# One kernel of two transformer blocks: buffers moved to multiples of 128 bytes, the context's weights kept 64 bytes further on

## The reference, cut to what matters

```python
for l in range(DEPTH):                       # first block, x is (1, 512, 1024)
    h = rmsnorm(x, mix_norm[l]); p = h @ w_in[l]
    ... attention, pool_mixer, sg_mixer ...
    x = x + mix @ w_o[l]
    h = rmsnorm(x, ffn_norm[l])
    x = x + (silu(h @ w_gate[l]) * (h @ w_up[l])) @ w_down[l]
...
for l in range(DEPTH):                       # second block, ctx is (1, 256, 1024)
    y_ctx, y_lat = mixer_ab(...) if l % 2 == 0 else mixer_c(...)
    x = x + g1 * rmsnorm_2(y_lat, norm_g[l, 1])
    x = x + g2 * rmsnorm_2(swiglu(modulate(x, ...), ffn_w_in[l], ffn_w_out[l]), norm_g[l, 3])
    if l < DEPTH - 1:
        ctx = ctx + ...                      # the same two steps for the context
```

## Time and profile before

| | |
|---|---|
| median of 3 runs | 3122.15 us (3119.57 to 3127.41) |
| profiled execution, its own time | 3127.66 us |
| its span, first to last instruction | 3125.9 us |
| instructions | 41566, of them 16448 matmuls |
| mean granted TensorE clock | 0.987 of full speed |
| TensorE busy | 3051.4 us, 98% of the span |

### The profile page before, as it was taken

The page is one execution under the profiler, slowest core; times in us unless marked ns, Lnnn a source line. Parts: engine busy times, 40 slices in busy tenths (PEclk is TensorE's granted clock), DMA queues, the critical chain, the costliest instruction groups (busy, mean ns, idle before and its releaser), DMA issues.

```text
span 3125.9 us, 41566 instructions
## 1 busy us (share of the span) xinstructions
PE 3051.4 (98%) x16448; PEld 2544.5 (81%) x16448; DVE 1718.9 (55%) x2894; ACT 1188.3 (38%) x1834; POOL 1237.6 (40%) x584
## 2 busy tenths in 40 slices
PE   8999999999999999999999999999999999999999
PEld 7658888887589888778888998878888789878887
DVE  4645676845563653665337866666675457441113
ACT  4543222235544432324336655542123435432222
POOL 4214444532157333334344454444444330144442
PEclk9999999999999999999999999999999999999999
DMA  8204554622135222223333333445553210123331
GB/s 131 64 28 123 174 160 126 197 71 64 45 109 170 85 83 88 79 70 101 115 101 98 116 112 108 135 131 166 184 156 118 89 59 10 41 71 101 98 94 68
DMA packets 480434, 323.88 MB, mean 104 GB/s; under 512 B 102520, under 2 KB 447744, under 8 KB 479728
## 3 DMA queue, kind: packets, MB, share of 16 engines
q1 hardware_dynamic: 475472, 309.60, 33.9%
q10 hardware_dynamic: 2656, 6.30, 0.5%
q0 software_dynamic: 2112, 5.32, 0.5%
HBM read 315.90 MB, written 5.24 MB: 103 GB/s over the span
## 4 chain that ended last, share of the span: by engine, by line
PE 90%; DVE 6%; ACT 2%; issue 1%; POOL 1%; DMA 0%; DVEq 0%; ACTq 0%; POOLq 0%
PE G L2950 13%; PE G L2959 12%; PE G L2960 12%; PE G L2964 12%; PE G L3179 6%; PE G L3180 6%; PE G L3184 6%; PE G L2977 3%; PE G L4082 1%; PE G L3396 1%; PE SS L3307 1%; PE G L3386 1%; PE G L3733 1%; PE G L3333 1%; PE MM L3307 1%
## 5 line engine op out<-in xcount | busy, mean ns | idle before, releaser
L756 POOL TENSOR_TENSOR WL<-raw,WH 128x1024 fp32r<-128x1024 f32 (+1 forms) x520 | 1194.5, 2320 | 1760.7 <-ACT WH L827 1760.5
L827 ACT ACTIVATE WH<-raw 128x1024 fp32r<-128x1024 f32 (+1 forms) x520 | 492.5, 995 | 597.4 <-PE G L3184 404.6
L2959 PE MATMUL G<-hH,WH 128*128 128x512 f32 x1520 | 595.1, 392 | 0.7 <-ACT xtok L1559 0.7
L2960 PE MATMUL G<-hL,WH 128*128 128x512 f32 x1520 | 591.9, 389 | 0.0
L2964 PE MATMUL G<-hH,WL 128*128 128x512 f32 x1520 | 359.9, 389 | 0.0
L2959 PEld LDWEIGHTS G<-hH,WH 128*128 128x128 f32 x1520 | 285.4, 188 | 61.4 <-ACT xtok L1559 0.9
L2964 PEld LDWEIGHTS G<-hH,WL 128*128 128x128 f32 x1520 | 285.3, 188 | 59.2
L2960 PEld LDWEIGHTS G<-hL,WH 128*128 128x128 f32 x1520 | 285.5, 188 | 58.5
L1755 DVE SCALAR_TENSOR_TENSOR acc<-adaw,cvec,acc 128x512 f32<-128x512 f32 x280 | 281.9, 1059 | 4.2
L1779 DVE TENSOR_TENSOR FH<-silu,G 128x512 fp32r<-128x512 f32 x44 | 30.3, 688 | 245.7 <-PE G L2964 191.2
L2950 PE MATMUL G<-hH,WH 128*128 128x512 f32 (+1 forms) x416 | 161.3, 388 | 0.0
(11 more groups left out here) (826 smaller groups left out, 6113.6 us busy)
## 6 DMA issues: line engine op xcount, KB each, us to landing
raw<-ffn_w_in_in SPq DMA_DIRECT2D x264, 256.0 KB, 3.4
adaw<-ada_w_in SPq DMA_DIRECT2D x48, 1024.0 KB, 5.3
raw<-ab_w_in_in SPq DMA_DIRECT2D x128, 256.0 KB, 3.0
raw<-ffn_w_out_in SPq DMA_DIRECT2D x96, 256.0 KB, 3.0
raw<-w_gate_in SPq DMA_DIRECT2D x88, 256.0 KB, 3.4
raw<-w_up_in SPq DMA_DIRECT2D x88, 256.0 KB, 3.4
raw<-w_down_in SPq DMA_DIRECT2D x64, 256.0 KB, 2.9
raw<-w_in_in SPq DMA_DIRECT2D x40, 256.0 KB, 3.4
```

The source lines that it names most:

```text
L756: nc.gpsimd.tensor_tensor(WL[c % 2][:, cut], raw[c % 2][:, cut], WH[c % 2][:, cut].bitcast(F32), ALU.subtract)\
L827: nc.scalar.activation(WH[c % 2][:, cut], raw[c % 2][:, cut], ACT.Copy).then_inc(weights_hi, 1)
L2959: mm(dst, view(WH[c % 2], k), high, start=(k == 0 and not (joint and i)), stop=False)
L2960: mm(dst, view(WH[c % 2], k), low, start=False, stop=False)
```

## The change

Three things are done to places, and none to the work or to its order.

1. `WH[0]`, `WH[1]` and `WL[0]` get 32 more columns (128 bytes a partition), `WL[1]` 16 more (64 bytes). All that `keep` places behind them moves: `WH[1]` by 128 bytes, `WL[0]` by 256, `WL[1]` by 384, and `sq`, `ht`, `rstd`, `ncol`, `ident` and all the others by 448.
2. The arena is rounded up to 128 in place of 64: it starts at 130176 = 1017 x 128. All in it moves by 448 bytes and now starts on a multiple of 128. The pass `m` and `xtok` are placed 128 bytes further on in it. `sq`, `ht` and `rstd` now start 64 past a multiple of 128, `ident` on one.
3. The chunks of all passes whose name begins with c or k (`c.ab`, `c.ab12`, `c.ab13`, `c.gu`, `c.dn`, `c.o`, `k.kv`) are written by ScalarE and GpSimd, and read by TensorE, 16 columns (64 bytes) further on in `WH` and `WL`. `raw` is used as before.

```diff
+APART = 32
...
-        WH = [keep(f"WH{s}", [P, SLOT], F32R) for s in range(2)]
-        WL = [keep(f"WL{s}", [P, SLOT], F32R) for s in range(2)]
+        WH = [keep(f"WH{s}", [P, SLOT + APART], F32R) for s in range(2)]
+        WL = [keep(f"WL{s}", [P, SLOT + APART // (1 + s)], F32R) for s in range(2)]
...
-        arena = (cursor[0] + 63) // 64 * 64
+        arena = (cursor[0] + 127) // 128 * 128
...
-        PM = Pass("m", T, lasting)
+        PM = Pass("m", T, lasting + 128)
...
-        xtok, _ = lay(lasting + 28 * 1024, ("xtok", [P, 4, D], F32))
+        xtok, _ = lay(lasting + 28 * 1024 + 128, ("xtok", [P, 4, D], F32))
...
+        beside = {first[name] + i for name, n, _ in names if name[0] in "ck" for i in range(n)}
+
+        def high(c):
+            return WH[c % 2][:, APART // 2:APART // 2 + SLOT] if c in beside else WH[c % 2][:, 0:SLOT]
+
+        def low(c):
+            return WL[c % 2][:, APART // 2:APART // 2 + SLOT] if c in beside else WL[c % 2][:, 0:SLOT]
...
-                        nc.gpsimd.tensor_tensor(WL[c % 2][:, cut], raw[c % 2][:, cut], WH[c % 2][:, cut].bitcast(F32), ALU.subtract)\
+                        nc.gpsimd.tensor_tensor(low(c)[:, cut], raw[c % 2][:, cut], high(c)[:, cut].bitcast(F32), ALU.subtract)\
...
-                    nc.scalar.activation(WH[c % 2][:, cut], raw[c % 2][:, cut], ACT.Copy).then_inc(weights_hi, 1)
+                    nc.scalar.activation(high(c)[:, cut], raw[c % 2][:, cut], ACT.Copy).then_inc(weights_hi, 1)
...
-                return lambda k: (view(WH[c % 2], k), view(WL[c % 2], k))
+                return lambda k: (view(high(c), k), view(low(c), k))
```

More of the change, by code:

```diff
@@ L2957, in streamed @@
                     for k in range(K):
-                        high, low = X(k)
-                        mm(dst, view(WH[c % 2], k), high, start=(k == 0 and not (joint and i)), stop=False)
-                        mm(dst, view(WH[c % 2], k), low, start=False, stop=False)
+                        xh, xl = X(k)
+                        mm(dst, view(high(c), k), xh, start=(k == 0 and not (joint and i)), stop=False)
+                        mm(dst, view(high(c), k), xl, start=False, stop=False)
                 pe.wait_ge(weights_lo, 2 * c + 2)
@@ L2963, in streamed @@
                     for k in range(K):
-                        last = mm(dst, view(WL[c % 2], k), X(k)[0], start=False, stop=(k == K - 1 and not (joint and i == 0)))
+                        last = mm(dst, view(low(c), k), X(k)[0], start=False, stop=(k == K - 1 and not (joint and i == 0)))
                     last.then_inc(pe_done, did("pe", mark))
@@ L3169, in lowered @@
             def lowered(c, outs, count, X, lows, joint=False):
-                part = lambda w, k, cols, o: w[c % 2][:, k * cols + o:k * cols + o + P]
+                part = lambda w, k, cols, o: w[:, k * cols + o:k * cols + o + P]
                 pe.wait_ge(weights_hi, 2 * c + 2)
@@ L3177, in lowered @@
                         for k in ks:
-                            high, low = X(k)
-                            mm(dst, part(WH, k, cols, o), high, start=(k == 0 and not (joint and i)), stop=False)
-                            mm(dst, part(WH, k, cols, o), low, start=False, stop=False)
+                            xh, xl = X(k)
+                            mm(dst, part(high(c), k, cols, o), xh, start=(k == 0 and not (joint and i)), stop=False)
+                            mm(dst, part(high(c), k, cols, o), xl, start=False, stop=False)
                 pe.wait_ge(weights_lo, 2 * c + 2)
@@ L3183, in lowered @@
                     for k in range(count):
-                        last = mm(dst, part(WL, k, cols, o), X(k)[0], start=False, stop=(k == count - 1 and not (joint and i == 0)))
+                        last = mm(dst, part(low(c), k, cols, o), X(k)[0], start=False, stop=(k == count - 1 and not (joint and i == 0)))
                     last.then_inc(pe_done, did("pe", mark))
```

## The result

| | before | after |
|---|---|---|
| median of 5 runs each | 3124.67 us (3119.57 to 3134.85) | 3144.93 us (3142.44 to 3147.52) |
| ratio | | 1.0051, 95% interval 1.0030 to 1.0072 |
| span of the profiled execution | 3125.9 us | 3142.9 us |
| mean granted TensorE clock | 0.987 | 0.986 |

The kernel became slower by 0.5%, where 0.4% faster was forecast (the quotient of the two medians alone is 1.0065, inside the interval of the ratio). The granted clock is nearly the same, 0.987 and 0.986; by an estimate from these figures that could be some 3 us, not 17. The page of the kernel after: the span; each engine's busy time; the chain's shares.

What follows compares the result with a forecast made beforehand. TensorE, busy 98% of the span, was taken as the bound, its pace set by operand places. 5.0 + 1.3 + 6.8 = 13.1 us gained, from the runs' median 3122.15 to 3109.0 us; range 3101 to 3122 us.

Steps and rivals of the forecast that it cites:

- the first reading: TensorE's matmul groups split by operand places modulo 128: 512 columns fastest both at 0, 256 columns fastest 64 bytes apart.
- what stays as it is: `cH`, latents' chunks over `hH`, `k.kv`, transposes, narrow products and the other engines: no gain or loss, 0 us.
- slot 1 is worse off: Rival: with a pattern of 256 bytes or more, odd chunks' latents' products lose 22 us; 3134 us, chance 0.09.
- The evidence against that rival: Scores' `c_kL` and `j_qH`, an odd multiple of 128 apart, take 120 ns like the pair at distance 0.
- The arena, 512 columns: `FH`, `t_FH`, `m_FH` products over weights, 2112 in all, 2.4 ns faster each: 5.0 us gained.
- Small groups: First block's queries' and keys' products and the scores, 336 matmuls at about 4 ns: 1.3 us gained.
- The context at 64: 1776 context matmuls of 256 columns go from 120.0 to 115.5 ns: 8.0 us, 6.8 kept.
- the 85%: Share of the context's 8.0 us counted as kept beside the latents' recurrence, given waits on VectorE: 6.8 us.
- the recurrence: Rival: VectorE's chain paces 1670 to 2010 us, leaving the context some 1 us; 7.3 us gained, 3115 us, chance 0.12.
- the three waits: TensorE's waits on VectorE in the context's stretch, 8.3 us of 340, where gain could be given back.
- Places don't matter: Rival: something other than operand places sorts the groups, so nothing changes; 3122 us, chance 0.11.

Runs made afterwards that it cites:

- experiment 5: Even chunks start 0 to 256 bytes further on in their slot, in turn, odd ones stay; one profiled execution of 3141.7 us, used for paces alone.
- experiment 1: Against the kernel before: all four weight buffers, `hH` and the arena congruent modulo 256, context's chunks 64 bytes further on in both slots; 3114.76 us, ratio 0.9956.
- experiment 3: The kernel before with the arena alone moved, to be congruent with the slots modulo 256; 3125.13 us, ratio 0.9988.
- experiment 4: The kernel before's distances modulo 256, with only `c.gu`, `c.dn` and `c.o` 64 bytes further on in both slots; 3118.86 us, ratio 0.9971.
- experiment 2: The kernel before with the change's wider `WH` and `WL` alone, nothing written further on, arena left at 192 modulo 256; 3150.74 us, ratio 1.0069.
- experiment 7: The kernel before with `WH` and `WL` of both slots 128 bytes further on, arena kept modulo 256; 3170.38 us, ratio 1.0127.
- experiment 9: The kernel before with small buffers 96 bytes off, no chunk moved, weight-to-activation distances unchanged modulo 256; 3129.26 us, ratio 0.9999.

## Why the prediction was wrong, point by point

- **The step that failed** is the first reading, where the groups were split by "where the two operands of the code lie, modulo 128 bytes". The period is 256 (experiment 5). Modulo 128 the change leaves the latents' products at "0 and 0", and the prediction put them at nothing under "what stays as it is"; modulo 256 it moves those of slot 1 to 128, where they take 232.5 ns in place of 227.1. That cost is 18.1 us against the 13.1 that were to be gained.
- **The rival "slot 1 is worse off"** is what happened; it had 0.09. Its 3150 products are there: 3144 with 512 columns over `hH` and `hL` lie at d = 128. Its price of 7 ns was too high: it is 232.5 - 227.1 = 5.4 ns, and 5.4 x 3144 = 17.0 us, where the sums show 18.1. It decided from 4.2 ns on, and 5.4 is above that.
- **The evidence against that rival** was the pair `c_kL` and `j_qH` at 120 ns, an odd multiple of 128 apart. That row is right and says little: at 256 columns 0 and 128 hardly differ (119.8 and 119), at 512 they differ by 5.4. The prediction noted that the row has 256 columns, and weighed it nevertheless. It also says that no row there has 512 columns, but the last line of the earlier trace rows, `j_kL` over `j_qH`, has: it lies 128 off, and the next start comes 230 ns later, as it does after `j_kH` over `j_qH`, which is at d = 0.

```profile
2612.47 0.28 PE L4111 MATMUL MM<-c_kH,j_qL 128*128 128x256 f32 x1
```

Over the 32 steps of the scores the two have medians of 230 ns (d = 128) and 232 (d = 0). In such streams, where widths alternate, the distances don't separate, so the row was no evidence for either side. What spoke for a longer period stood in its own rows: 512 columns at "64 and 0" took 229, at "0 and 64" 234.

- **The arena, 512 columns (5.0 us gained).** Nearly right with the places right: 3.9 us in experiment 1, and 4.3 in the usual products of experiment 3, of which 2.9 stayed. In the change half of these products went to 227 ns (runs of 12 in 2.89 us) and half to 233 (2.95 and 2.96), so the groups stayed at 392 and the sum rose by 2.5.
- **Small groups (1.3 us).** Not earned: `cqH` over `WH` is listed with 397 after 396.
- **The context at 64 (8.0 us, 6.8 kept).** The pace was right for slot 0 alone: 115.5 was taken, and it is 114.6 to 115.7 there and 117.8 in slot 1, 116.4 over both. That is 5.0 us by pace for the 1584 products over `c_nH` and `c_FH`, and 3.2 with the longer ones. The value taken lay between two levels that single chunks have (113 to 114, and 118), and 14 of the 22 chunks over `c_nH` were on the slow one. Experiment 4 kept 7.7 of 8.9, so the 85% was fair, and the recurrence isn't what takes the rest: the three waits of the earlier trace rows add up to 7.7 us there and 7.5 in the kernel after, against 8.3.
- **What stays (0).** `cH` stayed at 280, and the other engines' busy times are those of before.
- **Places don't matter** is refuted by experiments 1, 2 and 7. The Trainium skill (TensorE: Matmul & The Clock Gate, Part 2, the step on LDWEIGHTS), which gives TensorE two independent read ports, does not cover this: four bytes of distance take a 512-column product from 227.1 to 232.5 ns (experiment 5).

With the 18.1 and 2.5 us lost and 3.2 and 1.2 gained, 16.2 of the 17.0 us are accounted for; the rest is in products without weights and in the gaps. The range ended at 3122 us, where nothing is gained; the prediction gave slower a chance of 0.07 and left it out of the range.

Open are three things. The first is which stationary operand counts. While a product moves, the weights of the next one are loaded, and in most streams both stationary operands are congruent. Where the chunk changes they differ. In the kernel after, the last product of 57 chunks has its own weights at d = 0 and the next ones at 128, and takes 232.6 ns; in the kernel before such last products, with both at 0, take 226.6 (76 of them). So the next weights' place counts. The other way round, own at 128 and next at 0, they take 233.1 (50 of them), so the next place alone doesn't set the pace.

The second is why 256 columns are slowest at d = 0 and 512 columns fastest, and what picks between the two levels of 256 columns; neither was tested.

The third is the 15 more of the context's products above 126 ns in the kernel after. Their number is 74 in experiment 1, 84 in experiment 4 and 94 in experiment 9, and experiment 9 has all distances of before. So the distances need not be behind them, but one profile of each kernel doesn't show what is.

## What to carry to other kernels

On a kernel whose TensorE is the bound, place both operands of an fp32r product with 512 columns a multiple of 256 bytes apart, in every slot of a rotating buffer, and keep those with 256 columns off distance 0 (64 bytes here); here that was worth 0.44% (experiment 1), and padding one slot by 128 bytes cost 0.69% (experiment 2). When rows are sorted by a remainder, sort them by twice and four times that modulus before trusting it: two rows that should agree and differ (229 and 234) are worth more than a dozen that do agree. And a row of another shape is no evidence for this one.

## What the runs showed of the hardware that was not expected

The pace of back-to-back fp32r matmuls depends on the distance of the two operands' starts modulo 256 bytes: 227.1 ns at 0 and 232.4 to 234.2 between 4 and 160 bytes, then 229.0 at 192, 233.3 at 224 and 227.5 at 240, for 512 columns. These are streams of products over weights; those of the scores, in which widths alternate, did not follow it. It isn't symmetric: 64 bytes ahead cost 6.3 ns, 64 behind 1.9. With 256 columns the order is another one: 119.8 ns at 0, and 64 bytes to either side chunks at 113 to 114 ns beside chunks at 118, at the same distance modulo 256. The one chunk of the sweep over `c_nH` at 64 bytes was at 118.
